# The head of a two-block transformer kernel: input pairs alternate with quarters of the first weight unit, and TensorE runs four constant products first

## The reference, cut to what matters

```python
h = rms_norm(x, g_mix_pre[i])          # x / sqrt(mean(x*x) + eps) * g
proj = h @ w_in[i]                     # (256, 1024) @ (1024, 2048)
```

## Time and profile before

| | |
|---|---|
| median of 3 runs | 922.36 us (921.16 to 922.42) |
| profiled execution | 923.63 us |
| its span, first to last instruction | 921.8 us |
| mean granted TensorE clock | 0.994 |

### The profile page before, as it was taken

How to read it: one execution, slowest core, us unless ns; L and a number is a source line. 1 busy time by engine, 2 the same in 40 slices (tenths; PEclk the granted TensorE clock), 3 DMA queues, 4 the chain that set the end, 5 groups by cost and what they waited for, 6 DMA issues and landing times.

```text
span 921.8 us, 18183 instructions
## 1 busy us (share of the span) xinstructions
PE 894.4 (97%) x6786; PEld 846.6 (92%) x6786; DVE 674.2 (73%) x1113; ACT 507.3 (55%) x750; POOL 128.3 (14%) x81
## 2 busy tenths in 40 slices
PE   5999899999999999999999999989999999999997
PEld 5977799999999999889999999989889999999996
DVE  5975797777777847888766676878767787668665
ACT  6345644434435545876555555565378665555552
POOL 1000100000000023002223320302030023234003
PEclk9999999999999999999999999999999999999999
DMA  8853275565554654445555565542234375555541
GB/s 308 320 210 114 69 226 189 182 202 181 180 186 138 226 168 157 136 138 182 184 192 179 175 198 178 163 145 93 92 115 137 106 237 175 192 183 181 182 137 46
DMA packets 44147, 156.74 MB, mean 170 GB/s; under 512 B 5082, under 2 KB 5573, under 8 KB 43973
## 3 DMA queue, kind: packets, MB, share of 16 engines
q1 hardware_dynamic: 42336, 152.17, 50.6%
q10 hardware_dynamic: 1317, 2.35, 0.7%
q0 software_dynamic: 448, 1.59, 0.5%
HBM read 155.02 MB, written 1.06 MB: 169 GB/s over the span
## 4 chain that ended last, share of the span: by engine, by line
PE 88%; DVE 4%; ACT 4%; issue 1%; POOL 1%; DMA 1%; SPq 0%; DVEq 0%; POOLq 0%
PE ps L400 20%; PE ps L401 20%; PE ps L402 20%; PE ps L445 5%; PE ps L447 5%; PE ps L446 5%; PE ps L417 2%; PE ps L424 1%; PE ps L418 1%; DVE w_lo L1310 1%; PE ps L505 1%; PE ps L507 1%; PE ps L523 1%; PE ps L506 1%; POOL tok_rinv L297 1%
## 5 line engine op out<-in xcount | busy, mean ns | idle before, releaser
L400 PE MATMUL ps<-op_hi,w_hi 128*128 128x258 f32 (+1 forms) x1372 | 390.7, 285 | 0.9 <-DVE op_lo L1460 0.9
L402 PE MATMUL ps<-op_hi,w_lo 128*128 128x258 f32 (+1 forms) x1372 | 388.1, 283 | 0.0
L401 PE MATMUL ps<-op_lo,w_hi 128*128 128x258 f32 (+1 forms) x1372 | 387.9, 283 | 0.0
L1310 DVE TENSOR_TENSOR w_lo<-raw,w_hi 128x1024 fp32r<-128x1024 f32 x224 | 288.0, 1312 | 28.5 <-ACT w_hi L967 27.0
L967 ACT ACTIVATE w_hi<-raw 128x1024 fp32r<-128x1024 f32 x224 | 231.7, 1053 | 75.9 <-PE ps L402 44.4
L400 PEld LDWEIGHTS ps<-op_hi,w_hi 128*128 128x128 f32 x1372 | 260.5, 190 | 4.3 <-issue 1.3
L401 PEld LDWEIGHTS ps<-op_lo,w_hi 128*128 128x128 f32 x1372 | 261.4, 191 | 2.0
L402 PEld LDWEIGHTS ps<-op_hi,w_lo 128*128 128x128 f32 x1372 | 260.2, 190 | 0.0
L962 ACT ACTIVATE w_hi<-raw 128x1024 fp32r<-128x1024 f32 x60 | 63.4, 1057 | 62.1 <-PE ps L402 31.6
L400 PE MATMUL ps<-mix_hi,w_hi 128*128 128x256 f32 x304 | 87.1, 287 | 0.0
L1307 DVE SCALAR_TENSOR_TENSOR w_lo<-raw,row_mean,w_hi 128x1024 fp32r<-128x1024 f32 x60 | 78.9, 1316 | 10.0 <-ACT w_hi L965 9.9
(11 more groups left out here) (262 smaller groups left out, 1064.7 us busy)
## 6 DMA issues: line engine op xcount, KB each, us to landing
raw<-in_stream SPq DMA_DIRECT2D x284, 512.0 KB, 3.5
x<-in_x SPq DMA_DIRECT2D x4, 256.0 KB, 5.7
bias<-bias_rows POOLq DMA_DIRECT2D x1, 1024.0 KB, 8.1
work<-in_last_norm SPq DMA_DIRECT2D x1, 1024.0 KB, 5.7
result<-y SPq DMA_DIRECT2D x4, 256.0 KB, 2.0
spans<-in_spans ACTq DMA_DIRECT2D x1, 576.0 KB
bias<-bias_rows POOLq DMA_DIRECT2D x1, 512.0 KB, 11.4
proj<-in_gmask ACTq DMA_DIRECT2D x1, 512.0 KB
```

What stands on the lines that cost most here:

```text
L400: pe.matmul(o, wh, xh, start=start, stop=False, **kw)
L401: pe.matmul(o, wh, xl, start=False, stop=False, **kw)
L402: return pe.matmul(o, wl, xh, start=False, stop=stop, **kw)
L1310: m = dve.tensor_tensor(w_lo[:, s, :], raw[:, s, :], fp(w_hi[:, s, :]), ALU.subtract)
```

## The change

The loading, splitting and use of unit 0 go by quarters of 256 columns (128 KB, 1024 bytes to a partition; two input chunks' worth), and each alternates with the input pair that it meets. SP issues pair 0, quarter 0, pair 1, quarter 1 and so on, then units 1 to 5. ScalarE makes `op_hi` of pair i, then the hi part of quarter i; VectorE makes the lo part of quarter i, then `op_lo` of pair i. TensorE's new `first_unit` does unit 0 alone: 8 matmuls hi with hi and 16 others, each behind a wait for its own quarter or pair; unit 1 is then a plain `out_chunk` of 24 matmuls. Before all that TensorE waits for the constants of GpSimd and runs four float32 products of `mean_w` with itself, 384 columns each, into PSUM bank 5, which nobody reads.

```diff
--- before.py
+++ after.py
@@ -188,7 +188,7 @@
 
         names = """vec_loaded consts_loaded late_loaded pool_const table_ready table_copied table_stored bias_loaded
             pair_scored pair_read pair_shift pair_exp pair_scaled pair_turned pair_copied pair_summed v_turned
-            split_hi_done split_done units_done sq_ready sq_summed mean_done
+            split_hi_done split_done units_done first_hi first_lo sq_ready sq_summed mean_done
             stat_done var_ready tok_rinv_ready spread_done x_ready norm_hi operand_ready z_ready centred evac
             row_sq_ready row_var_ready alpha_ready last_loaded row_root_ready rows_dve rows_act rows_turned
             pooled pool_mixed mix_ready conv_done gate_act h_ready scaled
@@ -200,6 +200,7 @@
         S = {n: sem(n) for n in names}
         raw_loaded = [sem(f"raw_loaded_{s}") for s in range(SLOTS)]
         EV_IN, EV_EVEN, EV_ODD = 0, 14, 14 + 19
+        first_loaded = [sem(f"first_loaded_{i}") for i in range(3)]
         x_loaded = [sem(f"x_loaded_{i}") for i in range(4)]
         STATISTICS = (2, 2, 2, 2, 4, 8, 2)
         x_mean_sb = x_sum[:, 1, :]
@@ -218,6 +219,10 @@
 
             return t[:, 2 * i:2 * i + 2, :]
 
+        def quarter(t, i):
+
+            return t[:, 0, i * 256:i * 256 + 256]
+
         def bank2(b):
             return ps[:, b, :].rearrange("p (c t) -> p c t", c=2)
 
@@ -252,10 +257,10 @@
         @block.sync
         def _(sp):
             sp.dma_start(vec[:], d["vec"]).then_inc(S["vec_loaded"], 16)
-            sp.dma_start(pair(x, 0), pair(d["x"], 0)).then_inc(x_loaded[0], 16)
-            sp.dma_start(raw[:, 0, :], d["stream"][0]).then_inc(raw_loaded[0], 16)
-            for i in range(1, 4):
+            for i in range(4):
                 sp.dma_start(pair(x, i), pair(d["x"], i)).then_inc(x_loaded[i], 16)
+                sp.dma_start(quarter(raw, i), d["stream"][0][:, i * 256:i * 256 + 256]
+                             ).then_inc(first_loaded[i] if i < 3 else raw_loaded[0], 16)
             for s in range(1, SLOTS):
                 sp.dma_start(raw[:, s, :], d["stream"][s]).then_inc(raw_loaded[s], 16)
             rounds = UNITS // SLOTS
@@ -401,11 +406,33 @@
                 pe.matmul(o, wh, xl, start=False, stop=False, **kw)
                 return pe.matmul(o, wl, xh, start=False, stop=stop, **kw)
 
+            def first_unit(o, hi, lo):
+
+                for k in range(NCH):
+                    if k % 2 == 0:
+                        pe.wait_ge(S["norm_hi"], k // 2 + 1)
+                        pe.wait_ge(*((S["first_hi"], k // 2 + 1) if k < 6 else (S["split_hi_done"], 1)))
+                    w = slice(k * P, k * P + P)
+                    pe.matmul(o, w_hi[:, 0, w], hi[:, k, :], start=k == 0, stop=False)
+                    if k % 2:
+                        pe.wait_ge(*((S["first_lo"], k // 2 + 1) if k < 6 else (S["split_done"], 1)))
+                        for j in (k - 1, k):
+                            pe.matmul(o, w_lo[:, 0, j * P:j * P + P], hi[:, j, :], start=False, stop=False)
+                for k in range(NCH):
+                    if k % 2 == 0:
+                        pe.wait_ge(S["operand_ready"], k // 2 + 1)
+                    m = pe.matmul(o, w_hi[:, 0, k * P:k * P + P], lo[:, k, :], start=False, stop=k == NCH - 1)
+                given(m)
+
             def first_chunks(o, p, operand, hi=op_hi, lo=op_lo):
 
                 slots = (unit.n % SLOTS, (unit.n + 1) % SLOTS)
 
-                for part in (((0,), (1,)) if operand == 0 else ((0, 1),)):
+                if operand == 0:
+                    first_unit(o, hi, lo)
+                    out_chunk(p, hi, lo)
+                    return
+                for part in ((0, 1),):
                     pe.wait_ge(S["split_done"], unit.at(part[-1] + 1))
                     for k in range(NCH):
                         if k % 2 == 0:
@@ -656,6 +683,10 @@
                 if c >= 4:
                     pe.wait_ge(S["evac"], EV_IN + c - 3)
                 if c == 0:
+                    pe.wait_ge(S["pool_const"], 3)
+                    for _ in range(4):
+                        pe.matmul(bank(5, 0, 3 * P), mean_w[:, 0, :], mean_w[:].rearrange("p a b -> p (a b)"),
+                                  start=True, stop=True)
                     first_chunks(chunk(0, 0), chunk(1, 0), 0)
                 elif c > 1:
                     out_chunk(chunk(c % 4, 0))
@@ -1140,8 +1171,10 @@
                 for c in (2 * i, 2 * i + 1):
                     m = act.activation(op_hi[:, c, :], x[:, c, :], ACT.Copy, scale=vcol("g_mix_pre", c))
                 m.then_inc(S["norm_hi"], 1)
-                if i == 0:
-                    split_hi()
+                act.wait_ge(first_loaded[i] if i < 3 else raw_loaded[0], 16)
+                act.activation(quarter(w_hi, i), quarter(raw, i), ACT.Copy
+                               ).then_inc(S["first_hi" if i < 3 else "split_hi_done"], 1)
+            split.n += 1
             for _ in range(3):
                 split_hi()
             for i in range(4):
@@ -1633,14 +1666,16 @@
 
 
             for i in range(4):
+                dve.wait_ge(*((S["first_hi"], i + 1) if i < 3 else (S["split_hi_done"], 1)))
+                m = dve.tensor_tensor(quarter(w_lo, i), quarter(raw, i), fp(quarter(w_hi, i)), ALU.subtract)
+                m.then_inc(S["first_lo" if i < 3 else "split_done"], 1)
                 hi_n[0] += 1
                 dve.wait_ge(S["norm_hi"], hi_n[0])
                 for c in (2 * i, 2 * i + 1):
                     m = dve.scalar_tensor_tensor(op_lo[:, c, :], x[:, c, :], vcol("g_mix_pre", c), fp(op_hi[:, c, :]),
                                                  ALU.mult, ALU.subtract)
                 m.then_inc(S["operand_ready"], 1)
-                if i == 0:
-                    split_lo()
+            split.n += 1
             for _ in range(3):
                 split_lo()
             sum_squares(0)
```

## The result

The changed kernel takes 924.03 us (median of 20 runs, 923.0 to 926.7) beside 922.35 us before (20 runs): ratio 1.0021, 95% interval 1.0014 to 1.0028. It is slower by 1.7 us where I had forecast 0.3 faster, and the median lies just outside my range (921.1 to 923.8). I had called 1.8 us the least that can be told from no change; with 20 runs on each side the interval tells 1.7 from none. The profiled execution took 924.64 us, its span is 922.8, the mean granted clock 0.992.

The account below looks back on a forecast made before the run. PE, busy 97% of the span, was taken as the bound, starting late and slowly in the head, with the sum for `square_mean` limiting the gain. 0.5 us less 0.2 of transfer delay gave 0.3: 922.36 to 922.1, range 921.1 to 923.8.

Parts of the forecast that it names:

- The delay of the transfers: SP's queue in the head: unit 0's smaller packets make everything behind quarter 3 land 0.2 us later, range 0 to 1.5.
- The price of a packet: Unit 0's quarter transfers: 48 ns for each packet of 1024 bytes, against about 165 ns for one of 4096.
- these bytes don't change: Queue ahead of unit 1: the same bytes stand there, so issuing it at 5.6 instead of 3.89 us is covered.
- What the delay does: Head, up to `square_mean`: unit 3's landing sets the sum, which has about 0.5 us in hand and moves with the delay.
- my own formula: Gain at the end is 0.5 us less the transfers' delay: 0.5 with none, a loss of 1.0 with 1.5.
- The clock: Rival, PE in the head: clock falls in the new wait or among unit 0's bursts, giving 923.8 or 923.0; chance 0.2.
- since busy bursts raise it too: PE on unit 0: busy bursts raise the clock too, so failing constant products cost at most the clock rival's price.
- The issues: SP's queue: three more issues at 0.58 us each delay unit 1's issue by 1.74, covered; as rival 923.6, chance 0.06.
- ScalarE and VectorE: Splitting by quarters: hi part 0.46 us, lo part 0.42; ScalarE free at 11.0, last op_lo at 12.3, costing nothing.
- my estimate from its figure: Unit 0's small transfers at the skill page's lower bandwidth: 0.52 MB takes 3.8 us instead of 1.3, kernel ends at about 924.4.

Follow-up runs that it names:

- e13: The changed kernel measured again, unchanged: 923.92 us, ratio 1.0009.
- e16: The changed kernel without the four constant products, run again (repeat of e1): 923.72 us, ratio 1.0013.
- e5: The changed kernel with unit 0's quarters read from a copy that lies quarter by quarter in HBM: 923.43 us, ratio 1.0008.
- e14: Repeat of e5, the changed kernel with quarters contiguous in HBM: 923.38 us, ratio 1.0006.
- e15: The changed kernel with quarters read from a copy of unit 0 whose rows lie 5120 bytes apart in HBM: 923.99 us, ratio 1.0007.
- e1: The changed kernel without the four constant products and their wait: 923.88 us, ratio 1.0017.
- e2: The kernel before, with unit 0 loaded in four transfers of 256 columns: 924.79 us, ratio 1.0020.
- e10: The changed kernel with unit 0 in one transfer, squares ahead of unit 3's split and no constant products: 922.58 us, ratio 0.9994.
- e17: The changed kernel with unit 0's rows 5120 bytes apart in HBM and no constant products: 923.12 us, ratio 1.0006.
- e18: e17 with the squares and their sums ahead of unit 3's split: 921.80 us, ratio 0.9991.
- e11: The kernel before, with the four constant products ahead of it: 923.27 us, ratio 1.0006.
- e8: The kernel before, with three more tiny transfers (16 bytes to a partition) ahead of unit 1: 922.90 us, ratio 0.9999.
- e3: The kernel before, with unit 0 in four transfers of 32 neighbouring partitions: 923.78 us, ratio 1.0014.
- e7: The kernel before, with unit 0 in four transfers of every fourth partition: 926.65 us, ratio 1.0038.
- e12: e7 with each transfer's rows read from a contiguous copy in HBM: 925.58 us, ratio 1.0029.

## Why the prediction was wrong

**The delay of the transfers was the step that failed.** I put it at "0.2 us of all engines", with an upper end of 1.5; unit 3 came 1.7 later (15.18 for 13.47; 1.9 in e13, 1.2 in e16). The price of a packet in it was nearly right: 48 ns forecast, 57 measured in the changed kernel and 47 to 53 elsewhere. By my own sum that makes (512 x 57 - 128 x 163) / 16 = 0.5 us, with 163 ns for the packets of 4096 bytes in the kernel before. What failed is the spreading of that cost over all 16 engines. A transfer is there when its last engine is done, and some engines fell about two microseconds behind: unit 0's last packet starts at 10.9 while unit 1's first starts at 8.3. With the pieces at another place in HBM the delay shrinks to 0.3 (e5), 0.75 (e14) or nothing (e15). The sum had no term for where the pieces lie. The line "these bytes don't change", true of the bytes, hid that each transfer now reads a narrow slice of every row. Why that makes engines lag stays open.

**What the delay does** was right in part. Unit 3's landing sets the sum, the sum had 0.5 in hand, and 1.7 - 0.5 = 1.2 us is the loss by my own formula; e1 and e16 measured 1.6 and 1.2 (0.0017 and 0.0013 of 922.6). But this agreement is partly luck: in none of the profiles with the full delay did PE wait for the sum. Unit 1 was late by as much as unit 3, its first products ran at half pace, and PE came to the last four records 0.2 to 0.4 us after the sum was there (19.9 for 19.50 in the changed kernel, 19.4 for 19.2 in e1, 19.2 for 19.05 in e16), in e13 1.7 us and in e2 2.5 us after it. Two paths of nearly equal length stood side by side, and the one I had not forecast was the longer. Where the delay was small and unit 1 ran at full pace, the sum decided as forecast: in e5 unit 1's last product starts at 16.42, the last four records wait for the sum until 18.16, and the table product stands at 18.69, where I had 16.35, 18.0 and 18.5.

**The clock** was rival, not forecast, with 0.2; it should have had more. In all nine profiles with constant products it fell between 9.9 and 13.8 us. The premise "since busy bursts raise it too" held in e10, e17 and e18, where, without constants, unit 1's products are 0.12 apart from their third on, and failed in e1 and e16, where the first eight or nine start 0.21 apart. In the changed kernel's profile the fall costs about 0.2 us: from the end of the sum to the table product it is 0.6 (e5, e14, e17), so 20.1 was to be had and 20.33 was measured. In e13, the same kernel, all 24 products of unit 1 ran at half pace, and the same reckoning gives 21.88 less 20.33, about 1.5 us. Over the 20 runs, the nine with a mean clock of 0.992 or less have a median of 924.64, the six with 0.995 or more 923.50. So my estimate for the clock's part of the median's 1.7 us is 924.03 less 923.50, 0.5 us; e1 against the changed kernel can't tell it from none. The Trainium skill, page TensorE: Matmul & The Clock Gate, section HAM oscillation, says that waits for transfers between bursts of products bring the clock down; the changed kernel's windows agree, with a fall at 10.6, behind bursts with waits of 0.5 and 0.6 us between them and within the next wait, of 1.65. In e11 and e17 it fell without such bursts just before.

**The issues** cost nothing (e8), and **ScalarE and VectorE** kept up: a quarter's hi part took 0.40, where I took 0.46, and its lo part 0.42, as taken. The page DMA: Bandwidth & Descriptors of the Trainium skill (Bandwidth, Measured) had warned against small transfers, and by my estimate from its figure the kernel would have ended at 924.4; the direction was right, but e15 has the same 128 KB transfers with no delay at unit 3 and e5 with 0.3 us, so the size of the transfers is not the reason here.

**The range** came from cases taken one at a time. The delay's upper end and the clock could come together, and did.

## What to carry to other kernels

Before a transfer is cut into column slices, look at the pitch of its rows in HBM: with slices of 1024 bytes at a pitch of 4096 among its transfers the queue moved 0.51 and 0.61 MB in 2 us (e13, e16), with the same slices at 5120 0.71 and 0.73 (e15, e17), and a copy with padded rows took the delay away, one with the slices stored in one piece most of it. When a transfer is cut, don't divide its extra cost by the number of engines: look when the last short packet starts, since everything behind waits for the slowest engine; here units 1 to 3 all came 1.7 us later. Constant products ahead of this kernel bought nothing, as the clock fell again behind them in all nine profiles; in the kernel before, the low clock was spent where the engine had to wait anyway.

## What was not expected of the hardware

Transfers of 512 KB cut by partitions, 32 at a time with rows of 4096 bytes, are slow whether the rows are neighbours (192 GB/s from 5 to 7 us in e3), every fourth (210 in e7) or contiguous in HBM (208 in e12), against 361 in the kernel before. And behind a stretch of 0.3 us of waiting with thin work around it the clock fell for over 3 us in e17 and e5, but not in e14, while in the kernel before twelve such records without a wait had no fall behind them.
